# Strassen's seven products for twelve pairs of projected tiles in a one-core hybrid attention and state-space layer

## The chip, the cores and the metric

The kernel runs on one core of one Trainium2 chip. The metric is the device time of one execution in microseconds (us). A core has TensorE (PE, with its weight loads shown apart as PEld), VectorE (DVE), ScalarE (ACT), GpSimd (POOL) and SyncE (SP), whose queue issues nearly all DMAs here. Each engine runs its own instructions in program order and waits on semaphores that the others count up.

## The reference, cut to what matters

```python
u = x * (1.0 + scale[:, None, :]) + shift[:, None, :]
proj = u @ w_in                       # (1024 x 1024) @ (1024 x 5328)
q_lat, kv_lat, z_attn, xbc, dt_raw, z_ssm = split_last(proj, IN_SPLITS)
o_attn = mla_branch(q_lat, kv_lat, ...) * silu(z_attn)
o_ssm = ssd_branch(xbc, dt_raw, z_ssm, ...)   # conv of 4 taps, silu, then 8 chunks of 128 tokens
mixed = concatenate([o_attn, o_ssm]) @ w_out
return layer_norm(DEEPNORM_ALPHA * x + gate * mixed, ln_g, ln_b)
```

All is float32. In `ssd_branch` each chunk of 128 tokens needs exponentials of cumulated decays, products with masks, and the state left by the chunk before it.

## The kernel before, in words

Every float32 product is made as three passes of a split operand: a high part (a copy rounded by ACT) and a low part (raw minus high, by DVE or POOL), high by high, high by low, low by high, summed in PSUM (`three`). The projection has 34 tiles of 128 columns of `w_in`. A tile is turned out for two halves of 512 tokens, each over 8 blocks of the contraction, so it is 2 x 8 x 3 = 48 matmuls of 128x128x512. Tiles 0 to 5 give latents, rope and dt; tiles 6 to 17 are the 12 `xbc` tiles, whose convolution of four taps is made by DVE (`conv`, L1630 to L1673) and whose SiLU is made by ACT; tiles 18 to 33 are 16 gate tiles (z), one for attention and one for the state-space branch per chunk.

The weights of a tile come by SP (`load_tile`, L426) into one of two buffers `wraw`; ACT makes `wh` (`high`, L1178) and POOL makes `wl` (`split_tile`, L661, one 128x1024 subtraction). The z tiles are used as filling work in the eight chunks of the scan: `chunk(c, (2, 6, 4))` on PE (L877) does 2 parts of 8 matmuls, turns the staged chunk (`t_ready`), does 6 parts, the first two y rounds (`y_pair(0)`), 4 parts, the later two y rounds (`y_pair(2)`) and the new states. A y round needs `g_ready`, which ends one of DVE's four rounds.

DVE's program order in a chunk (L1716 to L1752) is: copies of the turned tiles, `xdt`, rounds 0 and 1, the evacuation of y rounds 0 and 1, rounds 2 and 3, `xdte`, evacuations 2 and 3, the state, the copy of the next stage. One round (`ssd_round`, L1686) is: a 128x4 subtraction, a 128x4 copy, four 128x128 instructions that write the exponent's argument (`arg_ready`), the product `cts`, and the product `dec` by `cbs` once ACT has made the exponential (`dec_ready`). ACT's order in a chunk (L1282) is: for rounds 0 and 1 the exponential of the rows (`exp_rows`) and of the decays (`exp_decay`, which waits for `arg_ready`), then two gate halves, the next `wh`, then rounds 2 and 3, two gate halves, the next `wh`. POOL in a chunk: one tile's `wl`, `xd` from the stage and the skip weights once the last chunk's y has been stored (`y_out`), the other tile's `wl`.

After the projection come the eight attention heads and the output projection, which the change leaves in their order.

Of the kernel before, what the change touches and what calls it, by code (L numbers as in the profile page):

```python
# [31 lines left out]
P = 128  # L32
D = 1024
# [34 lines left out]
SERIAL = 26  # L68
SLOT = (0, 1, 2, 3) * 6 + (0, 1, 4, 5, 2, 3, 0, 1)
# [13 lines left out]
def build_layer(nc, x, c, pos, w_ada, b_ada, w_in, qg, w_qb, kvg, w_kvb, conv_w, conv_b, dt_bias,  # L83
# [5 lines left out]
    sco = nc.dram_tensor("attn_scratch", [HEADS, P, S], F32).ap()  # L89

    ctx = ExitStack()
    with ctx:
# [8 lines left out]
        def sem(name):  # L101
# [4 lines left out]
        (ident, ones, mask_qk, mask_ls, colv, modc, gate_b, dsk, dsr, dtb, alg, ccol, rcst, small), end_c = at(base, [  # L106
            ("ident", [P, P], F32), ("ones", [P, P], F32), ("mask_qk", [P, P], F32), ("mask_ls", [P, P], F32),
            ("colv", [P, NVEC], F32), ("modc", [P, 16], F32), ("gate_b", [P, D], F32), ("dsk", [P, NST], F32), ("dsr", [P, SSM_H], F32),
# [4 lines left out]
        limit = nc.sbuf_usable_end  # L113

        (xin,), _ = at(reg_a, [("xin", [P, CHUNKS, D], F32)])
        (cx,), e = at(reg_a, [("cx", [P, 13, S], F32)])
        assert e <= reg_b
# [5 lines left out]
        top = (limit - 3 * S * 4) // 64 * 64  # L123
        (csn, krh, krl), _ = at(top, [("csn", [P, S], F32), ("krh", [P, S], F32R), ("krl", [P, S], F32R)])

        (uh, ul, wraw, wh, wl, ost), b1 = at(reg_b, [
            ("uh", [P, KT, S], F32R), ("ul", [P, KT, S], F32R), ("wraw", [P, 2, KT, P], F32),
            ("wh", [P, 2, KT, P], F32R), ("wl", [P, 2, KT, P], F32R), ("ost", [P, 2, S], F32)])
        (acc, wada, uf, vrow), e = at(b1, [("acc", [P, 2, 3, 2 * P], F32), ("wada", [P, 4, KT, 2 * P], F32),
                                           ("uf", [P, 2, S], F32), ("vrow", [NVEC, P], F32)])  # L130
        assert e <= limit
        (qk, xr, rb), e = at(b1, [("qk", [P, LAT, S], F32), ("xr", [P, 2, S + 4], F32), ("rb", [P, 2, S], F32)])
        assert e <= top

        posi = nc.alloc_sbuf_tensor_at("posi", [P, S], I32, offset=reg_a + 11 * S * 4)
        ropex, ropes, turns, dtv, sqs, dtw = cx[:, 8, :], cx[:, 9, :], xr[:, 0, 0:S], cx[:, 11, :], cx[:, 10, :], rb[:, 1, :]
        (wrx, whx, wlx), e = at(reg_a + 8 * S * 4, [("wrx", [P, KT, P], F32), ("whx", [P, KT, P], F32R), ("wlx", [P, KT, P], F32R)])
        assert e <= reg_a + 11 * S * 4
        (stg, xdt, bdt, cbs, exa, cts, state, xd, cdv, dec, xdte), e = at(b1, [
            ("stg", [P, 13, P], F32), ("xdt", [P, D], F32), ("bdt", [P, B0 + 2 * P], F32),  # L140
            ("cbs", [P, 2 * P], F32), ("exa", [P, 2, HB], F32), ("cts", [P, 2, HB], F32), ("state", [P, D], F32),
            ("xd", [P, NST, P], F32), ("cdv", [P, 3, SSM_H], F32), ("dec", [P, 4, HB], F32), ("xdte", [P, D], F32)])
        assert e - (D + 4 * HB) * 4 >= b1 + (LAT * S + 2 * (S + 4)) * 4
        xdte_at = e - D * 4
        assert e <= top
# [10 lines left out]
        sint = nc.alloc_sbuf_tensor_at("sint", [P, S], F32, offset=top - S * 4)  # L156
        assert e <= top - S * 4 and top - S * 4 >= xdte_at
# [4 lines left out]
        slot_at = [reg_a + q * 2 * (MX + OW) for q in range(3)] + [reg_b, ta_at + 2 * S * 4, top - S * 4]  # L162
# [5 lines left out]
        (res, lgb, lbb, yn, bns, gm), e = at(reg_b + 28 * 1024, [  # L168
            ("res", [P, CHUNKS, D], F32), ("lgb", [P, D], F32), ("lbb", [P, D], F32), ("yn", [P, RT, D], F32),
            ("bns", [P, CHUNKS, 24], F32), ("gm", [P, RT, D], F32)])  # L170
# [51 lines left out]
        colv_mm = sem("colv_mm")  # L222
        colv_ready = sem("colv_ready")
        gate_in = sem("gate_in")
        gate_acc = sem("gate_acc")
        gate_mm = sem("gate_mm")
# [10 lines left out]
        w_split = sem("w_split")  # L237
        proj_ready = sem("proj_ready")
        proj_evac = sem("proj_evac")
        dt_v = sem("dt_v")  # L240
        dt_abs = sem("dt_abs")
        dt_log = sem("dt_log")
# [4 lines left out]
        ss_mm = sem("ss_mm")  # L247
# [10 lines left out]
        acum_out = sem("acum_out")  # L258
# [20 lines left out]
        pos_in = sem("pos_in")  # L279
        pos_read = sem("pos_read")  # L280
        csn_ready = sem("csn_ready")
        csn_arg = sem("csn_arg")
        kr_t = sem("kr_t")
        kr_swapped = sem("kr_swapped")
        kr_sum = sem("kr_sum")
        krh_ready = sem("krh_ready")
        kr_ready = sem("kr_ready")
# [44 lines left out]
        ln_in = sem("ln_in")  # L332
# [44 lines left out]


        @block.sync
        def _(sp):  # L380
            sp.dma_start(ccol[:], c[0].rearrange("(p t) -> p t", t=KT)).then_inc(c_in, 16)

            def small_inputs():
                for dst, src in (
                    (gate_b[:], b_ada[0, 2 * D:3 * D].partition_broadcast(P)),
                    (dsr[:], d_skip[0].partition_broadcast(P)),
                    (rcst[:], const_in),
                    *[(dst[o:o + 16], src[0].rearrange("(h a) -> h a", a=1))
                      for dst, src in ((dtb, dt_bias), (alg, a_log)) for o in range(DT0, P, 16)],
                ):  # L390
                    sp.dma_start(dst, src).then_inc(small_in, 16)
# [4 lines left out]
            def x_columns(k):  # L396
                sp.dma_start(xin[:, :, k * P:(k + 1) * P],
# [20 lines left out]
            small_inputs()  # L418
            sp.dma_start(posi[:], pos[0].partition_broadcast(P)).then_inc(pos_in, 16)
# [5 lines left out]
            def load_tile(p, col, wait):  # L425
                src = w3[:, :, bass.ds(address(col), P)]  # L426
                if wait is not None:
                    sp.wait_ge(w_split, wait)
                sp.dma_start(wraw[:, p], src).then_inc(w_in_sem[p], 16)

            def store_z(tile, p, i):
# [1593 lines left out]
```

## Time and profile before

| | |
|---|---|
| Time, median of 3 runs | 935.5 us (934.63 to 935.82) |
| Span of the profiled execution | 932.6 us, run times lie some 2.9 us above it |
| Granted clock of TensorE, mean | 0.996 of full |
| PE busy | 898.0 us, 96% |
| DVE, ACT, POOL busy | 672.0, 462.3, 216.4 us |
| DMA | 126.27 MB, mean 135 GB/s |

A matmul's row shows its latency, which overlaps the next one's: back to back they start closer together than they last. "Busy" of PE is the time covered by any of them. The releaser named behind an idle time is the last semaphore event by this profile.

### The profile page before, as it was taken

To read this page: it belongs to the slowest core of one execution; us is meant where nothing else is said; L and a number is where in the kernel's file an instruction comes from. 1 tells how busy PE (TensorE), PEld (TensorE's weight loads), DVE (VectorE), ACT (ScalarE), POOL (GpSimd) and SP (SyncE) were. 2 spreads that over 40 slices of the span, in tenths; PEclk is the share of its full clock that TensorE was granted. 3 is DMA by queue.
4 is the path that set the end of the run, shared out by engine and by line. 5 is a ranking of instruction groups with operands and counts; after the bars stand their busy time and mean duration, and the time that the engine had idled before them with its cause. 6 is when DMAs were issued, how large, how long until landed. Compare 5 with 4: busy or idle time off the path is not lost.

```text
span 932.6 us, 13480 instructions
## 1 busy us (share of the span) xinstructions
PE 898.0 (96%) x4737; PEld 747.7 (80%) x4737; DVE 672.0 (72%) x1078; ACT 462.3 (50%) x727; POOL 216.4 (23%) x116
## 2 busy tenths in 40 slices
PE   4999999999999999999989999999999999999995
PEld 3788778788878788877878888888888788888884
DVE  6977489966877677777656766766766758457977
ACT  3654243533544554346457667666675934323421
POOL 1022212322212122121561323413315000002412
PEclk9999999999999999999999999999999999999998
DMA  9973204411234424444660422431422549534611
GB/s 297 320 280 96 63 22 160 112 46 45 66 116 136 140 86 134 135 135 127 178 215 15 147 64 88 147 105 44 146 104 90 181 154 407 194 135 152 204 51 79
DMA packets 110044, 126.27 MB, mean 135 GB/s; under 512 B 10646, under 2 KB 84599, under 8 KB 110007
## 3 DMA queue, kind: packets, MB, share of 16 engines
q1 hardware_dynamic: 109600, 124.95, 41.5%
q10 hardware_dynamic: 406, 0.84, 0.3%
q8 instruction: 22, 0.36, 0.2%
q14 instruction: 16, 0.12, 0.0%
HBM read 93.98 MB, written 27.85 MB: 131 GB/s over the span
## 4 chain that ended last, share of the span: by engine, by line
PE 71%; issue 12%; DVE 6%; SPq 5%; ACT 3%; POOL 1%; DMA 1%; DVEq 0%; ACTq 0%; POOLq 0%
PE bank L856 17%; PE bank L755 13%; PE bank L757 12%; PE bank L756 12%; PE bank L994 3%; SPq L404 2%; PE bank L979 2%; PE bank L873 2%; PE bank L983 2%; PE bank L982 2%; PE bank L980 2%; PE bank L981 2%; POOL wl L664 1%; PE bank L910 1%; PE bank L875 1%
## 5 line engine op out<-in xcount | busy, mean ns | idle before, releaser
L664 POOL TENSOR_TENSOR wl<-wraw,wh 128x1024 fp32r<-128x1024 f32 x31 | 78.1, 2520 | 199.0 <-ACT wh L1182 199.0
L755 PE MATMUL bank<-uh,wh 128*128 128x512 f32 x272 | 107.9, 397 | 2.8 <-DVE ul L1534 2.2
L756 PE MATMUL bank<-ul,wh 128*128 128x512 f32 x272 | 106.1, 390 | 0.0
L757 PE MATMUL bank<-uh,wl 128*128 128x512 f32 x272 | 106.0, 390 | 0.0
L856 PE MATMUL bank<-uh,wh 128*128 128x512 f32 x256 | 102.7, 401 | 0.0
L856 PE MATMUL bank<-ul,wh 128*128 128x512 f32 x256 | 101.2, 395 | 0.0
L755 PE MATMUL bank<-owh,mxh 128*128 128x512 f32 x256 | 100.1, 391 | 0.0
L856 PE MATMUL bank<-uh,wl 128*128 128x512 f32 x256 | 99.9, 390 | 0.0
L757 PE MATMUL bank<-owh,mxl 128*128 128x512 f32 x256 | 99.7, 390 | 0.0
L756 PE MATMUL bank<-owl,mxh 128*128 128x512 f32 x256 | 99.7, 389 | 0.0
L1280 ACT ACTIVATE dec<-dec 128x512 f32<-128x512 f32 x32 | 20.3, 633 | 113.1 <-DVE dec L1695 113.1
L1365 ACT ACTIVATE prob<-bank,small 128x1024 f32<-128x1024 f32 (+3 forms) x64 | 47.5, 743 | 34.2 <-DVE small L1798 34.0
L1840 DVE TENSOR_TENSOR owl<-owr,owh 128x1024 fp32r<-128x1024 f32 x32 | 41.0, 1280 | 32.6 <-ACT owh L1408 32.6
L755 PEld LDWEIGHTS bank<-uh,wh 128*128 128x128 f32 x272 | 51.3, 189 | 15.0 <-DVE ul L1534 3.1
L1811 DVE TENSOR_TENSOR ptl<-bank,pth 128x512 fp32r<-128x512 f32 (+1 forms) x96 | 50.2, 551 | 16.2 <-ACT pth L1384 15.8
L757 PEld LDWEIGHTS bank<-uh,wl 128*128 128x128 f32 x272 | 51.2, 188 | 10.7
L756 PEld LDWEIGHTS bank<-ul,wh 128*128 128x128 f32 x272 | 51.2, 188 | 10.7 <-issue 0.5
L1408 ACT ACTIVATE owh<-owr 128x1024 fp32r<-128x1024 f32 x32 | 33.8, 1057 | 50.9 <-PE bank L757 34.8
L856 PEld LDWEIGHTS bank<-ul,wh 128*128 128x128 f32 x256 | 48.1, 188 | 12.5 <-issue 3.0
L856 PEld LDWEIGHTS bank<-uh,wh 128*128 128x128 f32 x256 | 48.1, 188 | 11.5 <-issue 1.7
L755 PEld LDWEIGHTS bank<-owh,mxh 128*128 128x128 f32 x256 | 48.1, 188 | 10.3 <-DVE mxl L1842 0.3
L757 PEld LDWEIGHTS bank<-owh,mxl 128*128 128x128 f32 x256 | 48.0, 188 | 10.1
(231 smaller groups left out, 2207.7 us busy)
## 6 DMA issues: line engine op xcount, KB each, us to landing
wraw<-in_w_in SPq DMA_DIRECT2D x33, 512.0 KB, 3.7
owr<-in_w_out SPq DMA_DIRECT2D x32, 512.0 KB, 4.6
wada<-in_w_ada SPq DMA_DIRECT2D x16, 512.0 KB, 6.0
dec<-acum_scratch SPq DMA_DIRECT2D x32, 256.0 KB, 3.8
proj_scratch<-ost SPq DMA_DIRECT2D x16, 512.0 KB, 4.7
xin<-in_x SPq DMA_DIRECT2D x8, 512.0 KB, 6.0
cx<-in_w_ada SPq DMA_DIRECT2D x1, 4096.0 KB, 16.7
ssm_scratch<-xd SPq DMA_DIRECT2D x8, 512.0 KB, 5.4
```

The lines of the kernel that those rows point to most:

```text
L404: sp.dma_start(wada[:, k % 4, :, part * P:(part + 1) * P], ada[:, :, part, k, :]).then_inc(ada_in[k % 4], 16)
L664: pool.tensor_tensor(wl[:, p], wraw[:, p], wh[:, p].bitcast(F32), ALU.subtract).then_inc(w_split, 1)
L755: pe.matmul(dst, ah, bh, start=start, stop=False)
L756: pe.matmul(dst, ah, bl, start=False, stop=False)
L757: return pe.matmul(dst, al, bh, start=False, stop=stop)
L856: mm = pe.matmul(bk(2 * p + n), a[:, p, k, :], b[:, k, n * HB:(n + 1) * HB], start=(k == 0 and q == 0), stop=(k == KT - 1 and q == 2))
L994: mm = pe.transpose(bk(4 + n % 2)[:, (t - t0) * P:(t - t0 + 1) * P], prob[:, i % 2, t * P:(t + 1) * P], ident[:])
L1280: act.activation(dec[:, r, :], dec[:, r, :], ACT.Exp).then_inc(dec_ready, 1)
L1365: act.activation(prob[:, i % 2, 0:n], score_view(i), ACT.Exp, bias=small[:, 8 + i % 2:9 + i % 2], accum_out=small[:, 12 + i % 2:13 + i % 2 ...
L1408: act.activation(owh[at][:], owr[q][:], ACT.Copy).then_inc(e_hi, 1)
L1811: dve.tensor_tensor(ptl[:, t0:t0 + w, q], bk(4 + n % 2)[:, 0:w * P].rearrange("p (t q) -> p t q", q=P), pth[:, t0:t0 + w, q].bitcast(F32), ...
L1840: dve.tensor_tensor(owl[at][:], owr[q][:], owh[at][:].bitcast(F32), ALU.subtract).then_inc(e_split, 1)
```

## The change

Products are made after Strassen's scheme for 12 pairs of tiles: the last 8 `xbc` tiles as 4 pairs (q = 0 to 3), and the z tiles of a chunk as one pair (q = 4 to 11). Tiles 0 to 9 stay as they were. A pair is a 2x2 block product: two halves of the contraction and the two tiles on the weight side; two halves of the contraction and the two halves of the tokens on the other. It has 7 products of 4 blocks x 3 passes = 12 matmuls each, 84 in all, where two tiles had 96. The differences of u are made once, by DVE, and split by ACT and POOL (`split_difference`, four of 128x2048). For each pair POOL makes four sums of weights and seven low parts, all 128x512, and ACT seven high parts.

Products 0, 2, 4 and 6 (counted from 0) add up in one PSUM bank, which ACT copies out between them; 3 and 5 do so in another; DVE adds products 1, 4 and 5 from PSUM to what ACT has copied. So PE waits, between products of a pair, for ACT's copies and DVE's additions:

```diff
+            def product(i, q, odd):
+                pe.wait_ge(pair_split, 7 * q + i + 1)
...
+                elif i == 2:
+                    pe.wait_ge(prod_copied, 4 * q + 1)
...
+                elif i == 4:
+                    pe.wait_ge(prod_copied, 4 * q + 2)
+                elif i == 5:
+                    pe.wait_ge(prod_copied, 4 * q + 3)
+                elif isinstance(q, int) and q < PAIRS_XBC:
+                    pe.wait_ge(prod_added, 3 * q + 2)
+                else:
+                    pe.wait_ge(prod_added, 3 * q + 1)
```

Here `prod_copied` 4q + 2 is the copy of product 2, and `prod_added` 3q + 1 in a z pair is the addition of product 4. PE's chunk becomes:

```diff
+                product(0, q, odd)
...
+                turn_stage(c)
+                if not first:
+                    product(1, q, odd)
+                product(2, q, odd)
+                product(3, q, odd)
+                product(4, q, odd)
...
+                y_pair(0, c)
+                product(5, q, odd)
+                product(6, q, odd)
+                y_pair(2, c)
+                if more:
+                    new_states(c)
```

ACT's chunk (in chunk 0 the copy of product 0 and the first high part stand ahead of the row exponentials):

```diff
+                exp_rows(0, c)
+                exp_rows(1, c)
+                if not first:
+                    act.wait_ge(z_out[0], 16 * c)
+                    copy_product(0, q, odd, ost[:, 0, halves[0]])
+                if more and not first:
+                    high_product(0, q + 1)
+                exp_decay(0, c)
+                exp_rows(2, c)
+                exp_rows(3, c)
+                exp_decay(1, c)
+                if more:
+                    high_product(1, q + 1)
...
+                copy_product(2, q, odd, ost[:, 0, halves[1]])
...
+                copy_product(3, q, odd, ost[:, 1, halves[1]])
+                if more:
+                    high_product(2, q + 1)
+                    high_product(3, q + 1)
+                exp_decay(2, c)
...
+                exp_decay(3, c)
```

It goes on with the small exponential, high parts 4 and 5, two gate SiLUs once all three additions are done, the SiLU of product 6 and high part 6. In the last chunk latents stand in place of high part 1. DVE's chunk:

```diff
+                ssd_round(0, c)
+                ssd_round(1, c)
...
+                ssd_round(2, c)
                 y_out_round(0, c)
                 y_out_round(1, c)
-                ssd_round(2, c)
                 ssd_round(3, c)
+                add_product(4, q, odd, ost[:, 1, halves[1]])
```

then `xdte`, the additions of products 1 and 5, evacuations 2 and 3 and the state. `cts` is written in place of the row exponentials, which have four buffers. POOL, for each pair, with `skip_rows` (the old `xd`) behind it in every chunk:

```diff
+                pool.tensor_tensor(s1, a21, a22, ALU.add).then_inc(pair_sum, 1)
+                pool.wait_ge(pair_sum, 4 * q + 1)
+                pool.tensor_tensor(s2, s1, a11, ALU.subtract).then_inc(pair_sum, 1)
+                split_product(0, q, a11)
+                pool.tensor_tensor(a11, a11, a21, ALU.subtract).then_inc(pair_sum, 1)
+                split_product(1, q, a12)
+                pool.wait_ge(pair_sum, 4 * q + 2)
+                pool.tensor_tensor(a12, a12, s2, ALU.subtract).then_inc(pair_sum, 1)
+                split_product(2, q, s2)
+                split_product(3, q, s1)
```

and low parts 4, 5 and 6. A low part waits for its high part. SP loads both tiles of pair q + 1 once low parts 5 and 6 of pair q are made.

Around this, memory is laid out anew. The convolved tiles go to memory outside the chip (`scx`) and each chunk's stage is loaded from there by SP, in place of DVE's copy; the rope tables, the split rope keys and the gate go there and back as well. Convolution uses four buffers. The last two `xbc` tiles end so on DVE, and the first z pair's weights follow on SP:

```diff
+                if q == PAIRS_XBC - 1:
+                    dve.wait_ge(prod_copied, 4 * q + 4)
+                    conv(j + 1, 0, P)
+                    conv(j, HB, S)
...
+                    dve.tensor_copy(stg[:, LAST_Y, :], conv_out(LAST_Y)[:, 0:P]).then_inc(stage_ready, 1)
+                    conv(j + 1, P, S)
...
+            store_conv(LAST_X)
+            store_conv(LAST_Y)
             with sp.Fori(0, CHUNKS - 1) as i:
...
+                load_pair(i + PAIRS_XBC + 1)
```

In pair q = 0 DVE makes five latent norms between the additions of products 1 and 4. At the end of the last chunk the latents are loaded and split once products 1 to 4 have freed the memory in which u stood.

## Rows read from the trace of the kernel before

**Rows 1.** The page's first part: span; busy time, share and instructions of each engine.
```profile
span 932.6 us, 13480 instructions
PE 898.0 (96%) x4737; PEld 747.7 (80%) x4737; DVE 672.0 (72%) x1078; ACT 462.3 (50%) x727; POOL 216.4 (23%) x116
```

**Rows 2.** Stretches of convolution and of chunks: length, busy time by engine, clock, DMA.
```profile
123.00:238.00 115.00, 114.42 (x502) 93.17 (x501) 93.33 (x59) 46.97 (x54) 27.88 (x11) 1.00 0.27 79
238.00:471.00 233.00, 231.39 (x1415) 186.48 (x1414) 167.82 (x352) 117.08 (x157) 60.27 (x28) 1.00 0.43 128
```

**Rows 3.** Timeline of PE in one chunk: start, duration, engine, line, operation, tiles.
```profile
354.85 1.04 PE L893 MATMUL bank<-ident,stg 128*128 128x128 f32 x8
...
356.42 0.48 PE L856 MATMUL bank<-ul,wh 128*128 128x512 f32 x1
...
367.18 0.39 PE L856 MATMUL bank<-uh,wh 128*128 128x512 f32 x1
...
369.40 0.50 PE L856 MATMUL bank<-ul,wh 128*128 128x512 f32 x1
```

**Rows 4.** Timeline of DVE in the same chunk and at the next one's start.
```profile
356.70 0.49 DVE L1718 COPY bdt<-bank 128x320 f32<-128x320 f32 x1 [2.24 <-PE bank L897]
...
358.63 1.79 DVE L1689 TENSOR_TENSOR cdv<-dec,bdt 128x4 f32<-128x4 f32 x1
...
360.46 1.14 DVE L1695 SCALAR_TENSOR_TENSOR dec<-dec,bdt,mask_ls 128x128 f32<-128x128 f32 x4
...
363.10 1.14 DVE L1695 SCALAR_TENSOR_TENSOR dec<-dec,bdt,mask_ls 128x128 f32<-128x128 f32 x4
...
386.12 0.49 DVE L1718 COPY bdt<-bank 128x320 f32<-128x320 f32 x1 [2.24 <-PE bank L897]
```

**Rows 5.** Timeline of POOL in the same chunk.
```profile
356.16 1.90 POOL L686 TENSOR_TENSOR xd<-stg,dsk 128x1024 f32<-128x1024 f32 x1 [14.84 <-DMA ssm_scratch<-xd]
358.01 2.39 POOL L664 TENSOR_TENSOR wl<-wraw,wh 128x1024 fp32r<-128x1024 f32 x1
```

**Rows 6.** Timeline of all engines in the last chunk, third round.
```profile
462.54 3.28 DVE L1695 SCALAR_TENSOR_TENSOR dec<-dec,bdt,mask_ls 128x128 f32<-128x128 f32 x4
...
463.25 2.42 POOL L699 TENSOR_TENSOR qll<-wraw,qlh 128x1024 fp32r<-128x1024 f32 x1 [3.50 <-ACT qlh L1329]
```

**Rows 7.** Timeline of all engines in the output projection.
```profile
854.58 1.54 DVE L1840 TENSOR_TENSOR owl<-owr,owh 128x1024 fp32r<-128x1024 f32 x1 [2.26 <-ACT owh L1408]
855.12 2.15 POOL L720 TENSOR_TENSOR yn<-yn,lbb 128x512 f32<-128x512 f32 x1
856.05 1.77 DVE L1842 TENSOR_TENSOR mxl<-mxr,mxh 128x512 fp32r<-128x512 f32 x1
```

**Rows 8.** POOL by line and shape: count, busy us, mean ns, idle before.
```profile
L693 POOL TENSOR_TENSOR hwl<-hwr,hwh 128x512 fp32r<-128x512 f32 x4 | 5.2, 1288 | 11.8 <-ACT hwh L1324 11.8
```

**Rows 9.** Timeline of ACT in the same chunk as rows 3.
```profile
364.28 0.63 ACT L1280 ACTIVATE dec<-dec 128x512 f32<-128x512 f32 x1 [1.49 <-DVE dec L1695]
364.93 1.28 ACT L1272 ACT_TABLE_LOAD   x1
366.22 1.09 ACT L1272 ACTIVATE ost<-bank 128x512 f32<-128x512 f32 x2
```

**Rows 10.** The page's DMA issues: transfer, queue, count, KB each, us to landing.
```profile
wraw<-in_w_in SPq DMA_DIRECT2D x33, 512.0 KB, 3.7
...
ssm_scratch<-xd SPq DMA_DIRECT2D x8, 512.0 KB, 5.4
```

**Rows 11.** Timeline of DVE in the convolution's opening.
```profile
129.90 2.61 DVE L1636 SCALAR_TENSOR_TENSOR cx<-xr,colv,cx 128x1024 f32<-128x1024 f32 x2
...
136.09 13.14 DVE L1645 RECIPROCAL rb<-rb 128x1024 f32<-128x1024 f32 x2 [2.26 <-ACT rb L1235]
149.27 6.44 DVE L1648 SCALAR_TENSOR_TENSOR qk<-qk,colv,rb 128x1024 f32<-128x1024 f32 x5
```

**Rows 12.** A stretch behind PE's last matmul, columns as in rows 2.
```profile
924.00:928.00 4.00, 0.00 (x0) 0.00 (x0) 3.86 (x7) 0.29 (x1) 0.32 (x1) 0.61 0.32 131
```

More of the change, by code:

```diff
@@ new lines, in _ @@
+            load_pair(0)
+            store_conv(0)
+            store_conv(1)
+            load_pair(1)
+            for i, t in enumerate((2, 3, 4, 0, 1)):
+                sp.wait_ge(lat_ready, i + 1)
+                sp.dma_start(scr[t], qk[:, t, :]).then_inc(y_out, 16)
+            store_conv(2)
+            store_conv(3)
+            for q in range(2, PAIRS_XBC + 1):
+                load_pair(q)
+                for j in range(2):
+                    store_conv(2 * q + j)
+            sp.wait_ge(decay_out, 96)
@@ L861, in y_pair @@
+            for q in range(PAIRS_XBC):
+                for i in range(7):
+                    product(i, q, q % 2 == 1)
             def y_pair(r0, c):
@@ L874, in y_pair, with turn_stage @@
                         for q in range(2):
-                            mm = pe.matmul(d[q], state[:, own[q]], cts[:, r % 2, of[q]], start=False, stop=True)
+                            mm = pe.matmul(d[q], state[:, own[q]], decays(r)[:, of[q]], start=False, stop=True)
                     mm.then_inc(y_ready, 1)
-            def chunk(c, fills):
-                parts = iter([(p, n, part) for p in range(2) for n in range(2) for part in range(3)])
-                assert sum(fills) == 12
-                def fill(count):
-                    for _ in range(count):
-                        p, n, part = next(parts)
-                        proj_part(p, n, part, 2 * c + 18 + p)
-                fill(fills[0])
-                pe.wait_ge(stage_ready, c + 1)
-                if not isinstance(c, int) or c > 0:
+            def turn_stage(c):
+                pe.wait_ge(stg_in, 16 * c + 32)
+                if isinstance(c, int) and c == 0:
+                    pe.wait_ge(stage_ready, 1)
+                else:
                     pe.wait_ge(state_new, c + 1)
@@ new lines, in copy_product, with conv_silu @@
+            def copy_product(i, q, odd, dst):
+                act.wait_ge(prod_ready, 7 * q + i + 1)
+                act.activation(dst, {0: bk(3) if odd else bk(0), 2: bk(3) if odd else bk(0), 3: bk(2),
+                                     6: bk(3) if odd else bk(0)}[i], ACT.Copy).then_inc(prod_copied, 1)
+            def conv_silu(j):
+                act.wait_ge(conv_done, j + 1)
+                act.activation(conv_out(j), conv_out(j), ACT.Silu).then_inc(silu_done, 1)
+            halves = [slice(n * HB, (n + 1) * HB) for n in range(NHALF)]
@@ L1259, in _ @@
[L1259 to L1272 removed]
+            high_difference(2)
@@ L1280, in exp_decay, with z_gates @@
                 act.activation(dec[:, r, :], dec[:, r, :], ACT.Exp).then_inc(dec_ready, 1)
-            def chunk(c, more):
-                exp_rows(0, c)
+            def z_gates(q, c, odd, n):
+                if n == 0:
+                    act.wait_ge(prod_added, 3 * q + 3)
+                    act.activation(ost[:, 0, :], ost[:, 0, :], ACT.Silu).then_inc(z_done, 1)
+                    act.activation(ost[:, 1, halves[1]], ost[:, 1, halves[1]], ACT.Silu)
+                else:
+                    act.wait_ge(prod_ready, 7 * q + 7)
+                    act.activation(ost[:, 1, halves[0]], bk(3) if odd else bk(0), ACT.Silu).then_inc(prod_copied, 1)
@@ L1297, in chunk @@
[L1297 to L1302 removed]
+                if more:
+                    high_product(1, q + 1)
+                else:
+                    act.wait_ge(prod_ready, 7 * PAIRS - 5)
+                    latent_high(0)
+                    latent_high(1)
+                copy_product(2, q, odd, ost[:, 0, halves[1]])
```

978 lines of the change are left out of this document (594 added, 384 removed).

## The prediction

> **What bounds the kernel now.** I read the first part of the page, then the busy times by stretch, then the timelines of one chunk. PE is busy 898.0 of 932.6 us [rows 1], and in the stretches that the change touches 114.42 of 115 and 231.39 of 233 us [rows 2]. No other engine comes near. So matmuls taken out are worth their whole pitch, as long as nothing that now hides behind them comes due. That second half of the sentence decides this case: the reader should look in the timelines for how much DVE, ACT and POOL have in hand behind each product, and what they do to each other.
>
> **What is removed.** 48 matmuls run from 356.42 to 367.18 us [rows 3]: 10.76 / 47 = 0.229 us each (the 0.39 of a row is latency). Twelve pairs lose 12 matmuls each: 144 x 0.229 = 33.0 us, 2.75 us a pair. With all else hidden the time would be 935.5 - 33 = 902.5 us. A product is 12 x 0.229 = 2.75 us. A chunk lasts 386.12 - 356.70 = 29.4 us now [rows 4] and its work on PE will be 26.7.
>
> **What is added.** POOL: 11 instructions of 128x512 for a pair in place of two of 128x1024. The nearest row gives 1.29 us for a subtraction of that shape [rows 8], so 14.2 us a pair, and in a chunk 1.90 more for the skip rows [rows 5]: 16.1, against some 6.7 now. ACT: the high parts cost the same columns, plus three copies and SiLUs of what was evacuated anyway; it has room. DVE: three additions of 512 from PSUM, less the copy of the stage. By share all this fits under 26.7 us. By lock it does not:
>
> *POOL and DVE exclude each other.* The 128x4 subtraction on DVE at 358.63 lasts 1.79 us, to 360.42, just as POOL's instruction ends at 360.40 [rows 4, 5]; a 128x128 one needs 1.14 / 4 = 0.29, so 1.6 or so of it is waiting. Four 128x128 instructions of one round last 1.14 us alone [rows 4] and 3.28 with a POOL instruction of 2.42 that got in between the third and the fourth [rows 6]. And they take turns: DVE's at 854.58 waits for POOL's first, POOL's of 855.12 waits for DVE and lasts 2.15 instead of 1.29, DVE's next one waits for that, 1.77 us [rows 7]. DVE's evacuation from PSUM runs beside POOL unhindered. So where POOL has a row of instructions ready, each short DVE instruction with both inputs in SBUF waits for one of them, about 1.2 us. DVE's four rounds take 4 x 2.64 = 10.6 us of such work (360.46 to 363.10 is one round [rows 4]); with POOL's 16.1 that is 26.7, the whole chunk.
>
> The Trainium skill (SBUF — State Buffer, "Who interferes with whom") has this as an exclusive lock between GpSimd and DVE instructions with two SBUF inputs, held for the whole instruction; it says that whoever issues first has it, and nothing of turns. Taken as a lock that costs only where instructions happen to meet, it would make this kernel rival B below; with the turns of rows 7 it makes the forecast.
>
> **A middle chunk, step by step**, from the end of the turned stage, T.
> PE has products 1 to 3 until T + 8.2; then product 4 waits for ACT's copy of product 2. In ACT's order that stands behind `exp_decay(1)`, which waits for the arguments of DVE's round 1, and behind high part 1. From DVE's first copy to the end of those arguments is 364.24 - 356.70 = 7.5 us today, the wait of 1.6 for POOL included [rows 4, 5]; that block stays, since POOL still waits for y's store, 5.4 us [rows 10], and so starts when the stage is turned. Exponential 0.63, high part and copy 0.55 each [rows 9]: copy 2 ends at T + 9.3, 1.1 us late. That much is sure. Now the turns: the next pair's weights have landed by then (3.7 us [rows 10] after low parts made at the end of the last chunk), so POOL goes from the skip rows straight into four instructions (two sums, low part 0, a difference) until it lacks high part 1. All four fall into rounds 0 and 1: 4 x 1.2 = 4.8 us. I take both ends' upper one here, since nothing else is left for POOL to do: stall 5.9 us.
> Product 6 waits for the addition of product 4, which now stands behind rounds 2 and 3 and the evacuation of y rounds 0 and 1. Without POOL: round 1 done T + 8.9, round 2 T + 11.6, first y rounds (1.99 us [rows 3]) end T + 14.1, evacuated 14.9, round 3 17.5, addition 18.2; PE is done with product 5 at 16.8: 1.4 us late. With four more turns (low part 1, a difference, low parts 2 and 3) it is 3.7; a part of them falls into DVE's wait for y, so I take 3.0.
> A middle chunk: 26.7 + 5.9 + 3.0 = 35.6 us, 6.2 more than now; six of them: +37.
>
> **Chunk 0.** Once pair 3's last product is done, DVE still has about one and a half convolutions in pieces (1.3 us for each of three steps of 1024 columns [rows 11], a whole one some 4.7), stage copies between: estimate 9.6 us, and SiLU 1. Only then SP may store that tile and fetch the next weights, 0.4 + 3.7 [rows 10]; ACT waits for these at high part 0, which stands ahead of the row exponentials. High part, table load 1.28, exponential [rows 9], two rounds' arguments 3.9, then exponential, high part, copy: 23.7 us. PE has four products and the turning, 12.6. Stall 11.1, plus turns 4.8, plus 3.0 at product 6, less 2.75: +16.2.
> **Chunk 7.** No next pair, but two latents of 1.1 us each (twice 0.55) ahead of copy 2: stall 2.5 + 2.0 - 2.75 = +1.8.
> **The way out.** Latents and their weights are split while PE runs products 5 and 6 only; the tables come from outside the chip. 0 to 8, I take 3.
>
> **The convolution's pairs.** Four save 11.0 us. In pair 0, product 6 needs DVE's addition of product 4, behind convolution 2, a reciprocal (6.6), convolution 3 and five norms, 6.4 [rows 11]: 23.8 us plus 3.5 until ACT gets to tile 8, against 27.5 that PE has (tile 9 and six products). It just fits; but eleven of DVE's instructions there can each lose a turn to POOL, which splits u's differences and two pairs in that time: 0 to 13.2, I take 10. Later pairs have slack of several us. Sum: -1.
>
> **Sum.** -1 + 16.2 + 37.2 + 1.8 + 3 = +57 us. Span 932.6 + 57.2 = 989.8; with the 2.9 by which the run lies above the profiled span, 992.7. The input stage and the attention keep their order: at nothing, covered by PE's unbroken work; In front of tile 6 DVE has the four differences of u (2.6 us each, estimate from the 1.3 for 1024 columns [rows 11]), ten steps of the rope tables (some 11), eight gate terms (10.4) and some 7 of dt and rope: 39 us, against tiles 2 to 5 on PE, 4 x 11.0 = 44. I take it as hidden; with POOL's turns it could cost some 5.
>
> **Rivals.**
> A, the forecast: turns at the lock on the way to copy 2. 993 us, chance 0.55.
> B, on the other side: POOL's instructions meet DVE's only by chance, so only the late copy and addition remain. Middle chunks 26.7 + 1.1 + 1.4 = 29.2 (-0.2 x 6), chunk 0 +9.8, chunk 7 +1.1, convolution -11, way out 0: -1.3 in all, 934 us. For it: DVE idles in places into which POOL may fall. Against it: rows 7. It decides from less than one lost turn a chunk on. Chance 0.18, in which faster and slower are about even.
> C, also on the other side: copies and additions come in time, the saving stays whole: 903 us. It would need ACT to reach copy 2 some 1.1 us before DVE's rounds let it. 0.15.
> D: the stalls of A let TensorE's clock fall. Behind the last matmul, at 922.7, the granted clock of 924 to 928 us averages 0.61 [rows 12], so it went to its lower level, 1.2 GHz, after some 2 us of rest. A product at that level costs 2.75 us more; in each of eight chunks, 22: 1015 us. 0.12.
>
> **Numbers.** 993 us. The range leaves out C and the far ends of B and D: 920 to 1025. A difference of 0.2% is about what a measurement of this kernel can tell. Faster by more: C and half of B, 0.23; within it 0.05; slower 0.72.
>
> **What would show it.** PE's longest waits: product 4 for ACT's copy, some 6 us each in chunks 1 to 6; then product 6 for DVE's addition, about 3. DVE's 128x128 and 128x4 instructions with means far above 0.3 us, POOL's 128x512 above 1.29. Chunks 35 to 36 us apart. Product 6 of the first pair late by some 10. In chunk 0 ACT waits for a weight load. Wrong would be: chunks of 29 us with those means undisturbed (B); no wait on `prod_copied` at all (C); a clock under 1 in the chunks (D); or a hole before tile 6 or the attention, which I have at next to nothing.

## The result: slower by 7.6%, and the profile after

| | before | after |
|---|---|---|
| Time, median | 935.7 us (934.63 to 935.82) | 1006.1 us (1004.05 to 1009.89) |
| Ratio, 95% interval | | 1.0759 (1.0734 to 1.0784) |
| Span of the profiled execution | 932.6 us | 1002.2 us |
| Mean granted clock | 0.996 | 0.963 |

After, first part of the page and its clock by slices (to be held against [rows 1]):

```profile
span 1002.2 us, 13509 instructions
PE 899.3 (90%) x4593; PEld 737.1 (74%) x4593; DVE 763.5 (76%) x1117; ACT 473.7 (47%) x785; POOL 386.2 (39%) x228
PEclk9999997899788999999998999999999999999998
```

144 matmuls fewer, and PE is busy as long as before: what it does runs slower in the middle. After, by stretch (length, busy time and count of PE, PEld, DVE, ACT, POOL, granted clock, DMA share, GB/s); against [rows 2]:

```profile
51.00:123.00 72.00, 71.91 (x309) 57.75 (x308) 65.29 (x50) 30.33 (x36) 29.47 (x11) 1.00 0.53 169
123.00:263.50 140.50, 116.97 (x475) 93.49 (x474) 115.83 (x79) 51.97 (x76) 106.17 (x59) 0.92 0.37 108
263.50:302.40 38.90, 27.95 (x156) 21.36 (x156) 26.98 (x48) 17.29 (x27) 15.83 (x11) 0.81 0.38 115
337.20:371.30 34.10, 28.91 (x169) 22.39 (x168) 28.38 (x47) 14.77 (x24) 18.20 (x12) 0.95 0.45 134
```

A chunk begins where DVE copies the turned tiles. By these marks the 69.6 us divide so:

| stretch | before | after | more | predicted |
|---|---|---|---|---|
| start to chunk 0 | 240.98 | 263.56 | +22.6 | -1 |
| chunk 0 | 27.5 | 38.8 | +11.4 | +16.2 |
| chunks 1 to 6 | 6 x 29.42 | 6 x 34.2 | +28.8 | +37 |
| from chunk 7 on | 487.6 | 494.6 | +6.9 | +4.8 |

(Chunk 0's mark stands behind 24 matmuls of its pair after and 16 of its tiles before, so some 1.8 us of the first line belong to the second.) Up to 123 us nothing is lost, as forecast: PE is busy 71.91 of 72.

PE's longest waits behind the input stage; the first two are those that the prediction named (engine, line, what for; us in all, times, longest):

```profile
PE bank L932 <- ACT ost L1435: 35.3, 8, 10.0
PE bank L932 <- DVE ost L1973: 11.3, 8, 3.6
PE bank L932 <- ACT xrb L1435: 9.6, 3, 5.9
PE bank L1091 <- DMA stg<-conv_scratch: 6.2, 1, 6.2
```

L1435 is ACT's copy of a product, L1973 DVE's addition. In a middle chunk product 4 waits 4.2 us for the first, product 6 waits 1.0 for the second. But a list of waits says who was waited for, not what it would bring to shorten one. That is in the chain of waits, followed back from the end. After, one chunk of it (start, us, what; some pieces, all under 1.3 us, are left out):

```profile
339.79 1.15 DVE dec L2031 x4
340.96 0.64 ACT dec L1545
342.24 1.26 DVE cdv L2025
343.60 4.20 DVE dec L2031 x4
347.82 0.64 ACT dec L1545
349.10 1.26 DVE cdv L2025
350.46 4.12 DVE dec L2031 x4
354.60 0.64 ACT dec L1545
356.79 1.15 DVE dec L2031 x4
357.97 0.64 ACT dec L1545
359.24 0.69 DVE ost L1973
359.98 0.50 PE bank L932
```

No product is in it before product 6, at 359.98: from the turned stage (337.17) on, the chain is DVE's four rounds, then the addition of product 4: 22.8 us. L2031 are the four 128x128 instructions of a round (the rounds are counted from 0): 1.15 us undisturbed, 4.2 in rounds 1 and 2, and the 128x4 copy ahead of them (L2025) 1.26 instead of 0.16. POOL in the same stretch:

```profile
341.72 1.75 POOL L821 TENSOR_TENSOR wxy<-wraw 128x512 f32<-128x512 f32 x1 [2.05 <-DMA wraw<-in_w_in]
343.55 1.29 POOL L823 TENSOR_TENSOR wxy<-wxy,wraw 128x512 f32<-128x512 f32 x1
344.80 1.32 POOL L814 TENSOR_TENSOR wl<-wraw,wh 128x512 fp32r<-128x512 f32 x1
346.08 1.31 POOL L825 TENSOR_TENSOR wraw<-wraw 128x512 f32<-128x512 f32 x1
349.05 1.28 POOL L814 TENSOR_TENSOR wl<-wraw,wh 128x512 fp32r<-128x512 f32 x1 [1.67 <-ACT wh L1430]
350.29 1.28 POOL L828 TENSOR_TENSOR wraw<-wraw,wxy 128x512 f32<-128x512 f32 x1
```

Eight instructions of POOL, in two rows of four (the last two, to 354.1, are not shown), beside two of DVE's rounds: two copies and two times four arguments lose 1.1 + 1.1 + 3.05 + 2.97 = 8.2 us, and 8.6 with the 0.4 that the skip rows cost the first copy. In each row one instruction of POOL holds up the copy and the next three hold up three of the four arguments. That is a turn of about 1.0 us for each instruction of POOL.

### The profile page after: what moved, and what is told of

Read it like the earlier page. It is cut to its first block, busy times and chain, and to the rows that moved or that the text cites. A ratio compares the mean times of both kernels' runs of the same rounds, so it can differ in the third digit from the quotient of the medians.

```text
span 1002.2 us, 13509 instructions
## 1 busy us (share of the span) xinstructions
PE 899.3 (90%) x4593; PEld 737.1 (74%) x4593; DVE 763.5 (76%) x1117; ACT 473.7 (47%) x785; POOL 386.2 (39%) x228
## 4 chain that ended last, share of the span: by engine, by line
PE 56%; DVE 23%; issue 6%; ACT 6%; SPq 4%; DMA 3%; POOL 2%; DVEq 0%; ACTq 0%; POOLq 0%
PE bank L932 14%; PE bank L934 14%; PE bank L933 14%; DVE dec L2031 8%; PE bank L1209 3%; DVE cvb L1954 2%; ACT dec L1545 2%; SPq L470 2%; DVE cdv L2025 2%; PE bank L1194 2%; PE bank L1198 1%; PE bank L1197 1%; PE bank L1195 1%; POOL diff_lo L804 1%; PE bank L1196 1%
## 5 line engine op out<-in xcount | busy, mean ns | idle before, releaser
L932 PE MATMUL bank<-uspan,wh 128*128 128x512 f32 x352 | 147.0, 418 | 18.2 <-DVE ost L1973 11.3
L934 PE MATMUL bank<-uspan,wl 128*128 128x512 f32 x352 | 139.6, 397 | 0.0
L814 POOL TENSOR_TENSOR wl<-wraw,wh 128x512 fp32r<-128x512 f32 x60 | 102.6, 1721 | 74.1 <-ACT wh L1430 74.1
L933 PE MATMUL bank<-uspan,wh 128*128 128x512 f32 x304 | 119.1, 392 | 0.0
L932 PE MATMUL bank<-diff_hi,wh 128*128 128x512 f32 x144 | 65.0, 451 | 46.6 <-ACT ost L1435 35.3
L932 PEld LDWEIGHTS bank<-uspan,wh 128*128 128x128 f32 x352 | 67.5, 192 | 40.6 <-issue 15.6
L2031 DVE SCALAR_TENSOR_TENSOR dec<-dec,bdt,mask_ls 128x128 f32<-128x128 f32 x128 | 83.9, 715 | 1.1
L933 PE MATMUL bank<-diff_lo,wh 128*128 128x512 f32 x192 | 84.4, 439 | 0.0
L934 PEld LDWEIGHTS bank<-uspan,wl 128*128 128x128 f32 x352 | 67.5, 192 | 15.0
L933 PEld LDWEIGHTS bank<-uspan,wh 128*128 128x128 f32 x304 | 57.6, 189 | 13.1 <-issue 2.2
L934 PE MATMUL bank<-diff_hi,wl 128*128 128x512 f32 x144 | 63.1, 438 | 0.0
L1430 ACT ACTIVATE wh<-wraw 128x512 fp32r<-128x512 f32 x60 | 36.3, 623 | 56.6 <-DMA wraw<-in_w_in 45.9
L1653 ACT ACTIVATE prob<-bank,small 128x1024 f32<-128x1024 f32 (+3 forms) x64 | 47.6, 744 | 32.4 <-DVE small L2145 32.1
```

The source lines that it names most:

```text
L814: pool.tensor_tensor(wl[:, at], part, wh[:, at].bitcast(F32), ALU.subtract).then_inc(pair_split, 1)
L932: pe.matmul(dst, ah, bh, start=start, stop=False, skip_group_check=running)
L933: pe.matmul(dst, ah, bl, start=False, stop=False, skip_group_check=running)
L934: return pe.matmul(dst, al, bh, start=False, stop=stop, skip_group_check=running)
L1430: act.activation(wh[:, PRODUCT_SLOT[i]], part, ACT.Copy).then_inc(pair_high, 1)
L1653: act.activation(prob[:, i % 2, 0:n], score_view(i), ACT.Exp, bias=small[:, 8 + i % 2:9 + i % 2], accum_out=small[:, 12 + i % 2:13 + i % 2 ...
```

## Experiments

The question after this reading was what bounds a chunk: the waits that one sees on PE (my sum), or the chain on DVE. Each kernel below was timed beside the kernel before on the same chip (medians of that 934.4 to 936.3); ratios are to it.

### Does the place of ACT's copy matter?

```diff
                 exp_rows(3, c)
+                copy_product(2, q, odd, ost[:, 0, halves[1]])
                 exp_decay(1, c)
...
-                copy_product(2, q, odd, ost[:, 0, halves[1]])
```

> ACT's copy of product 2 stands ahead of exp_decay(1) and of the next high part. Program-order theory (product 4 is late because of where its copy stands, as the sum of the prediction has it): the 4.2 us in front of product 4 go, in chunks 1 to 6 and in part in 0 and 7; with the slow clock behind it (about 1.7 us) that is some 5 to 6 us a chunk, 1006 becomes about 965. Chain theory (product 6 waits for DVE's addition of product 4, which ends 22.8 us after the turned stage whatever PE does, since DVE's rounds with POOL's turns fill that time): the idle time moves to the first y rounds and to product 6, chunks stay 34.1 us apart, 1003 to 1006.

1020.6 us, ratio 1.0906 (1.0882 to 1.0929): slower than after by 14 us, where both theories had it at 1006 or faster. PE in a chunk, and two windows (the chunk, and behind product 6's wait):

```profile
389.19 0.44 PE L1078 MATMUL bank<-dec,xdt 128*64 128x128 f32 x4 [0.63 <-DVE dec L2039]
399.93 0.79 PE L932 MATMUL bank<-uspan,wh 128*128 128x512 f32 x1 [6.71 <-DVE ost L1973]
376.65:414.00 37.35, 30.01 (x168) 23.27 (x167) 28.82 (x46) 14.87 (x24) 17.38 (x12) 0.86 0.39 122
402.00:406.00 4.00, 4.00 (x15) 2.77 (x15) 0.80 (x2) 2.12 (x4) 0.75 (x1) 0.50 0.26 105
```

The wait of 4.2 us is gone, and product 6 starts 23.3 us after the turned stage (22.8 in after): the program-order theory falls, the chain stands. What the chain theory didn't have is the loss. One rest of 6.7 us now stands in front of work that is on the chain, and that work, product 6 and the later y rounds, runs at a granted clock of 0.50, the level of 1.2 GHz: from product 6 to the next turned stage it takes 14.1 us here and 11.3 in after. In after, the rest that let the clock fall stood in front of product 4, which had time.

### Are the turns bound to the rounds, or to chance?

```diff
+                if not (isinstance(q, int) and q <= PAIRS_XBC):
+                    pool.wait_ge(arg_ready, 4 * (q - PAIRS_XBC) - 2)
                 pool.wait_ge(w_in_sem[0], 16 * q + 80)
```

> POOL starts on the next pair's weights only when DVE has written the exponents' arguments of round 1. Turns theory: the four arguments of round 1 take 1.14 us again in place of 4.2, product 4 waits about 1.1 us in place of 4.2; but the same instructions of POOL now meet rounds 2 and 3, whose arguments take about 4.1 us each, and the addition of product 4 ends as late as before: product 6 waits some 4 us, chunks about 34 us apart, 1000 to 1010. Chance theory (a meeting costs only where two instructions happen to overlap): half the stretched instructions go and don't come back, chunks 30 to 31, about 985.

1019.1 us, 1.0887 (1.0867 to 1.0907). DVE's arguments of rounds 1 and 2, and product 6 of that chunk:

```profile
383.55 1.14 DVE L2033 SCALAR_TENSOR_TENSOR dec<-dec,bdt,mask_ls 128x128 f32<-128x128 f32 x4
388.27 5.14 DVE L2033 SCALAR_TENSOR_TENSOR dec<-dec,bdt,mask_ls 128x128 f32<-128x128 f32 x4
400.80 0.80 PE L934 MATMUL bank<-uspan,wh 128*128 128x512 f32 x1 [6.54 <-DVE ost L1975]
```

Round 1 is free (1.14), round 2 pays for both: its four arguments take 5.14 us, its products 1.77 and 1.75 instead of 0.69. Turns theory held in kind: nothing was given back. The size was missed (1000 to 1010 expected): all the waiting now gathers in one rest of 6.5 us, as in copy2_early.

### Is the low clock a cost of its own?

```diff
-                for k in range(4):
+                for k in [k for n in range(times) for k in range(4)]:
...
-                product(3, q, odd)
+                product(3, q, odd, 2)
```

> Product 3 is made twice in every chunk (its second pass starts the bank anew), so PE rests 1.4 instead of 4.2 us in front of product 4, with 12 more matmuls a chunk. If the lower TensorE clock is a term of the loss by itself (product 4 takes 4.5 us at a granted clock of 0.60 instead of 2.75): 1.7 us a chunk come back, 1006 becomes about 993. Chain theory: product 4 is back at 2.75 us, but product 6 still starts when DVE's addition is done, so its wait grows from 1.0 to about 2.7 us and chunks stay at 34.1: 1004 to 1006.

1008.1 us, 1.0771 (1.0753 to 1.0789), after plus 2 us: no gain. In the middle chunk:

```profile
339.00:373.20 34.20, 29.94 (x180) 23.47 (x179) 28.54 (x46) 14.77 (x24) 18.32 (x12) 1.00 0.42 133
361.99 0.50 PE L932 MATMUL bank<-uspan,wh 128*128 128x512 f32 x1 [2.63 <-DVE ost L1973]
```

The clock is back at 1.00, PE does 12 matmuls more, and the chunk lasts 34.2 us as before; product 6 waits 2.6 instead of 1.0. In after's chunks the slow clock costs nothing.

### What is POOL's work worth?

```diff
-                pool.tensor_tensor(wl[:, at], part, wh[:, at].bitcast(F32), ALU.subtract).then_inc(pair_split, 1)
+                f = cut(q)
+                pool.tensor_tensor(f(wl[:, at]), f(part), f(wh[:, at].bitcast(F32)), ALU.subtract).then_inc(pair_split, 1)
```

`cut` takes 8 of every 128 columns, in the four sums too; pair 0 stays whole. The kernel leaves out the other columns of sums and low parts.

> POOL's sums and low parts of pairs 1 to 11 are made for 8 of every 128 columns only; their number, order and semaphores stay. The rest of the weights' low parts is left out, so this isn't the reference's output. Turns theory: DVE's stretched instructions (8.6 us in a middle chunk beyond their time alone) go; the chain to the addition of product 4 is then 14.2 us and PE decides: 26.7 us plus about 1.1 in front of product 4 = 27.8, six times 6.3 less, with what chunks 0, 1 and 7 and the convolution's pairs give another 10 to 20: 945 to 960. If another wait bounds the chunk (the weight loads, ACT's order), chunks stay above 32 us and the time above 985.

951.9 us, 1.0160 (1.0138 to 1.0181): 54 us less than after. Arguments take 1.14 us again, and a middle chunk is:

```profile
343.14:371.55 28.41, 27.30 (x168) 21.27 (x167) 19.98 (x46) 14.68 (x24) 6.68 (x12) 1.00 0.53 157
```

28.4 us, and the stage of chunk 0 is turned 11.5 us earlier (248.5 against 260.0): POOL's columns cost 5.7 us in a chunk and 11.5 in the convolution. Three of POOL's instructions, of 0.25 to 0.30 us now, run beside DVE's four arguments of round 1, and these take 1.14 us all the same.

The other side of it is the old kernel with that load, 6 and 5 instructions of 128x512 for a chunk's two tiles, and nothing else of the change:

```diff
-                split_tile(0, 2 * i + 18)
+                split_pieces(0, 2 * i + 18, 9 * (i - 1), 6)
...
-                split_tile(1, 2 * i + 19)
+                split_pieces(1, 2 * i + 19, 9 * (i - 1) + 5, 5)
```

> The kernel before, with POOL making each later z tile's low part in pieces of 128x512, some of them again with the same result: 11 instructions of 128x512 for a chunk in place of two of 128x1024, the load on POOL of the change without its products, copies and additions. Turns theory: DVE's rounds 2 and 3 end 23.6 us after the turned stage (19.5 and 4.1 us of turns) where PE is ready for the later y rounds at 20.1: about 3.5 us a chunk, seven chunks, 936 becomes about 960. Chance theory: less than 1 us a chunk, 936 to 942.

982.4 us, 1.0498 (1.0481 to 1.0516): +47 us with not one product changed, where the turns theory expected 24 and chance at most 6. POOL's row, DVE's arguments of rounds 0 and 1 beside and behind it, PE in front of the later y rounds, and the chunk:

```profile
310.25 6.38 POOL L669 TENSOR_TENSOR wl<-wraw,wh 128x512 fp32r<-128x512 f32 x5
312.84 4.20 DVE L1708 SCALAR_TENSOR_TENSOR dec<-dec,bdt,mask_ls 128x128 f32<-128x128 f32 x4
318.54 1.14 DVE L1708 SCALAR_TENSOR_TENSOR dec<-dec,bdt,mask_ls 128x128 f32<-128x128 f32 x4
333.02 0.44 PE L886 MATMUL bank<-dec,xdt 128*64 128x128 f32 x4 [2.22 <-DVE dec L1719]
335.66 0.45 PE L886 MATMUL bank<-dec,xdt 128*64 128x128 f32 x4 [1.54 <-DVE dec L1719]
310.55:345.68 35.13, 31.37 (x180) 24.59 (x179) 26.98 (x45) 14.12 (x19) 15.80 (x13) 0.95 0.33 104
```

4.20 against 1.14 within two rounds of one chunk is the turn as plain as it gets. PE waits 2.2 + 1.5 = 3.8 us, as expected (3.5); on top the clock falls in front of the new states and the next tiles, which are on the chain: PE is busy 31.4 us in this chunk, and 32.1 on average of chunks 1 to 6 (which lie 35.8 apart), with what took 29.4 at full clock. That part the expectation lacked.

### Can the order be mended?

add4_early takes both waits out of the products' way, with copies 2 and 3 and the addition of product 4 made earlier:

```diff
+                add_product(4, q, odd, ost[:, 1, halves[1]])
                 ssd_round(2, c)
                 y_out_round(0, c)
                 y_out_round(1, c)
                 ssd_round(3, c)
-                add_product(4, q, odd, ost[:, 1, halves[1]])
...
+                copy_product(2, q, odd, ost[:, 0, halves[1]])
+                if not first:
+                    act.wait_ge(z_out[1], 16 * c)
                 exp_decay(1, c)
+                copy_product(3, q, odd, ost[:, 1, halves[1]])
```

> In every chunk copies 2 and 3 stand ahead of the next high parts (copy 2 ahead of exp_decay(1)) and DVE adds product 4 between rounds 1 and 2 instead of behind round 3. This takes product 6 off the chain through rounds 2 and 3. Chain theory: the addition ends about 13 us after the turned stage instead of 22.8, product 6 waits for nothing; what is late next is round 3 for the later y rounds, some 23.3 us after the turned stage against 19.4 of PE: a rest of about 4 us there, chunks 31.7 us apart (up to 33 if the lower clock falls on the work behind it), six times 1 to 2.4 less than 34.1: 990 to 1000. If the addition was not what bound the chunk, no change: 1004 to 1008; if the longer single rest costs clock as in copy2_early, above 1010.

989.5 us, 1.0581 (1.0563 to 1.0599), just under the 990 to 1000 that were expected: 16.7 us less than after. Chunks are 32.2 us apart on average (from 297.41 to 490.70, six); there the products wait no more, the y rounds do, for DVE's rounds. Two of its chunks:

```profile
362.39:397.18 34.79, 30.26 (x168) 23.07 (x167) 29.20 (x47) 15.25 (x25) 18.30 (x13) 0.90 0.49 162
397.18:427.05 29.87, 27.24 (x168) 21.36 (x167) 27.35 (x47) 14.38 (x24) 16.99 (x12) 1.00 0.36 119
```

The same code: 3.0 of the 4.9 us between them are PE's work at the lower clock.

chunk0_order, in chunk 0 alone:

```diff
                 if first:
                     copy_product(0, q, odd, ost[:, 0, halves[0]])
-                    high_product(0, q + 1)
...
                 exp_decay(1, c)
+                if first:
+                    copy_product(2, q, odd, ost[:, 0, halves[1]])
+                    high_product(0, q + 1)
```

> In chunk 0 alone ACT makes high part 0 of the next pair behind the exponentials of round 1 and behind copy 2, so the load of that pair's weights doesn't hold up the rows' exponentials. In after these stood behind a wait of 5.8 us, and product 4 waited 10.0. By the prediction's step for chunk 0: the wait goes to 2 to 4 us, chunk 0 lasts some 6 to 8 us less, 998 to 1000. Rival (DVE's rounds meet POOL's turns later and the addition of product 4 sets chunk 0's end too): 1 to 3 us kept, 1003 to 1005.

1005.5 us, 1.0750 (1.0722 to 1.0779), no difference that the time shows. In chunk 0 product 4's wait falls from 9.98 to 1.2 us, product 6's grows from 0.97 to 7.0: the rival, again a wait that moves to DVE's addition. From chunk 0 to chunk 7 it is 241.1 against 244.1 us.

Two orders for the convolution, which the prediction had at next to nothing. conv_order:

```diff
                 copy_product(0, q, odd, one[:, halves[0]])
+                copy_product(2, q, odd, one[:, halves[1]])
+                act.wait_ge(conv_done, LATE if q == 0 else j - 2)
+                copy_product(3, q, odd, two[:, halves[1]])
                 high_product(0, q + 1)
                 high_product(1, q + 1)
...
                 add_product(4, q, odd, two[:, halves[1]])
+                if q == 0:
+                    for t in (2, 3, 4, 0, 1):
+                        latent_norm(t)
```

> In the convolution's pairs ACT makes copies 2 and 3 ahead of the next pair's high parts 0 to 2, and DVE adds product 4 of pair 0 ahead of the five norms of the latents instead of behind them. Chain theory: product 6 of pair 0 started at 179.3 us because the norms (10.2 us with POOL's turns) stood ahead of that addition; it starts 8 us earlier now, the waits of 5.9 and 2.0 us go, but DVE's work up to the last convolution is the same and it has only some 15 us of holes in that stretch, so 4 to 8 us are kept: 998 to 1002. Rival (DVE and POOL are the bound of the whole stretch, not single waits): nothing is kept, 1005 to 1007, and the first stage is turned at 260 us as before. Rival 2 (the high parts were late already): the next pairs' low parts come late and it is slower than 1007.

1012.5 us, 1.0832 (1.0810 to 1.0855): 6 us more. What was saved in pair 0 came back in pair 1:

```profile
193.90 0.77 PE L932 MATMUL bank<-diff_hi,wh 128*128 128x512 f32 x1 [10.28 <-ACT xra L1435]
```

ACT's copy there waits for a buffer that DVE clears only once the latents are stored, and these came later.

opening, in the first pair:

```diff
-            for i in range(3):
+            for i in range(2):
                 high_product(i, 0)
             act.wait_ge(conv_done, 1)
             evac(8, conv_in(2)[:, 3:3 + S])
+            high_product(2, 0)
...
                 copy_product(0, q, odd, one[:, halves[0]])
+                if q == 0:
+                    copy_product(2, q, odd, one[:, halves[1]])
                 high_product(0, q + 1)
...
-                if isinstance(q, int) and q == 0:
-                    split_difference(3)
                 pool.wait_ge(pair_sum, 4 * q + 4)
                 split_product(5, q, a12)
                 split_product(6, q, a22)
+                if isinstance(q, int) and q == 0:
+                    split_difference(3)
```

> Three moves in the first pair of the convolution alone: ACT evacuates tile 8 ahead of high part 2 (which waited 6.3 us for POOL's second sum while DVE waited 4.2 us for that tile), POOL makes low parts 5 and 6 ahead of u's fourth difference (4.6 us, so the next pair's weights are fetched that much earlier), and ACT makes copy 2 ahead of the next pair's high parts, which waited 11.6 us for those weights. Chain theory: the waits of 3.0 and 5.9 us in front of products 2 and 4 of pair 0 fall to 0 and about 2, part of the lower clock behind them goes too, and 5 to 9 us are kept: 997 to 1001. Rival (DVE's norms in front of the addition of product 4, and the one set of weight buffers that each pair must free before the next can be fetched, keep the pace): product 6 of pair 0 and all later pairs stand where they stood, 1004 to 1007.

1008.9 us (1001.54 to 1010.45), 1.0758 (1.0714 to 1.0802): nothing. Product 6 of pair 0 starts at 181.8 (179.3 in after) and now waits 4.8 us for the addition behind the norms. Then the edits together: add4_early and chunk0_order, in all_orders with conv_order, in best_orders with opening in its place:

> The three edits of conv_order, chunk0_order and add4_early together. If each removes another stretch's chain they add up: 1006 less about 6, 7 and 12 = 981. With none of POOL's work taken away it stays well above the kernel before; if the gains overlap, 985 to 995.

> The edits of opening, chunk0_order and add4_early together. add4_early took 16.8 us off the eight chunks, chunk0_order 3.0; with 5 to 9 from the opening: 1006 less 25 to 29 = 977 to 981. If the opening gives nothing, 984 to 987.

995.3 us, 1.0654 (1.0637 to 1.0672), and 986.1 us, 1.0535 (1.0517 to 1.0553). conv_order costs in company too, 9 us against opening. best_orders, where opening gives nothing as before, is the fastest whole version, 20 us under after and 51 over before. Last, whether any such order could have won: best_orders, with POOL's columns left out as in pool_small.

> best_orders with POOL's sums and low parts of pairs 1 to 11 made for 8 of every 128 columns, as in pool_small: the rest of the low parts is left out, so this isn't the reference's output. It asks what the scheme could give if POOL's work cost DVE nothing. pool_small took 951.9 us; opening and orders take 5 to 9 us from its first pair and up to 1 us from each chunk of 28.4: 935 to 945, so no gain worth the name over the kernel before. If the three convolution pairs behind the first then run at PE's pace as well, 925 to 935.

937.4 us, 1.0020 (1.0005 to 1.0034). Two chunks of it:

```profile
304.79:331.49 26.70, 26.70 (x168) 21.43 (x167) 20.44 (x47) 14.75 (x24) 5.91 (x12) 1.00 0.48 161
331.49:358.19 26.70, 26.70 (x168) 21.42 (x167) 20.85 (x47) 14.93 (x25) 5.91 (x12) 1.00 0.58 177
```

26.70 against 29.42 us: here the saving stands whole, 2.72 us a pair. And still it is no gain: chunk 0 begins at 253.1 instead of 241.0, and behind the mark of chunk 7 it takes 498.0 us instead of 487.6.

## Where the prediction was right and where wrong

**Sign and main cause: right. Size: right with luck.** 993 was forecast, 1006 measured, inside the range. But chunks 0 to 6 had 53 us in the sum and measure 42, while the convolution had -1 and measures 21 or more; two errors in opposite directions make the total look better than its terms. The turns at the lock are shown from both sides: without most of POOL's columns 54 us go, and POOL's load alone, in the old kernel, brings 47 (the whole change brings 70, its saving of 33 taken off).

**The price of removed matmuls: right.** 2.75 us a pair forecast, 2.72 in best_small. Rival C needed nothing else to come due. best_small takes away most of POOL's work, and even so the rest of the change eats the gain.

**The middle chunk: right engine, wrong sum.** I forecast 35.6 us and it is 34.2. Product 4 waits 4.2 instead of 5.9: the four turns before it cost 4.1 us and not 4.8, and the skip rows hold up DVE for 0.4 and not 1.6, so that the copy would not be late without turns. Product 6 waits 1.0 instead of 3.0. The step that failed is the addition itself: 26.7 + 5.9 + 3.0 adds PE's waits as if each could be had back. Nor do the waits as measured give the chunk: 26.7 + 4.2 + 1.0 = 31.9, and the other 2.2 us are PE at its lower clock, busy 28.9 us with work of 26.7. The true account is one chain: 22.8 us from the turned stage to DVE's addition of product 4, then product 6, y rounds, new states, product 0 and the turning, 11.3. "That much is sure", of the copy 1.1 us late, was wrong: in pool_small, without turns, product 4 waits 0.2 to 0.3 us. Its opposite number, the addition of product 4 behind round 3, 1.4 by my steps, is 0.9 there. Rival B's chunk of 29.2 is 28.4.

**Rival D: the clock.** It did fall, to 0.60 in the stretch of product 4, which takes 4.5 instead of 2.75 us, behind a rest of 4.2; the "some 2 us of rest" that I read from rows 12 are not enough in a chunk, where a rest of 2.6 in warm leaves the clock at 1.00. Of its price, 22 us added to the forecast, warm leaves nothing in the chunks: the slow product sits beside the chain. The step that failed is again that it was added. Where a rest stands on the chain the price is real, as copy2_early (14 us) and before_pool (2 to 3 a chunk) show, and in the convolution after, below.

**Chunk 0: 13 with the share of the mark, for 16.2.** The wait in front of product 4 is 10.0 and ACT waits 5.8 us for weights, as described (the pieces that I listed for ACT's path add up to 22.8 us, not to the 23.7 that I used). Not in my steps: PE waits 6.2 us in front of the turning, ahead of chunk 0's mark and so in the first line of the table, since the stage now comes back from memory outside the chip, through the queue and two transfers. I had let DVE's copy of the stage go as a gain and priced its stand-in at nothing.

**The convolution: the term that was mis-sized, -1 forecast, +21 to +23 measured.** PE's account of 123 to 263.5 us: what it had to do, 117.4 less 11.0 plus 1.8 = 108.2; idle 23.5; the rest, 8.8, is PE at a clock of 0.92. Idle in pair 0:

```profile
155.46 0.50 PE L932 MATMUL bank<-diff_hi,wh 128*128 128x512 f32 x1 [2.98 <-ACT xrb L1435]
166.93 0.63 ACT L1430 ACTIVATE wh<-wraw 128x512 fp32r<-128x512 f32 x1 [11.61 <-DMA wraw<-in_w_in]
168.71 0.77 PE L932 MATMUL bank<-diff_hi,wh 128*128 128x512 f32 x1 [5.94 <-ACT xrb L1435]
168.41 10.18 DVE L1965 SCALAR_TENSOR_TENSOR qk<-qk,colv,rb 128x1024 f32<-128x1024 f32 x5
179.33 0.48 PE L932 MATMUL bank<-uspan,wh 128*128 128x512 f32 x1 [2.00 <-DVE xrb L1973]
```

I counted product 6 alone, at 10 us, and these rows are 10.9. So that term was right in size by luck, with the place wrong: over half of it, 5.9 us, is ACT's copy 2 behind a high part that waits for weights. What was missing is all else: "later pairs have slack of several us", which the lock ate (a convolution step of DVE's takes 2.17 us instead of 1.28 where POOL has work, the norms 10.18 instead of 6.44 [rows 11], and POOL's 128x512 beside the norms take 2.15 to 2.27 instead of 1.29, so here both sides pay; DVE is busy 115.8 of 140.5 us); the stage's 6.2; the clock. pool_small gives 11.8 us back of this stretch. That leaves some 11 for orders, transfers and clock, and neither of my two orders got any of it. Which wait holds it is open; both moved a wait to DVE's side, so I take DVE's whole row of work there as the likeliest bound, which was not shown.

**From chunk 7 on: +6.9 for 4.8.** Products 4 and 6 wait 1.4 and 3.6 us in chunk 7, and PE 0.9 and 1.1 later, at a latent's low part and at the attention's start; pool_small, which leaves the latents' split whole, takes as long here as after; the weights' lock beside the latents was not taken apart.

## What to carry to other kernels

Before adding up waits of the bounding engine, follow the chain of waits through one period and ask of every wait what would come next if it were gone: three of these experiments (copy2_early, pool_late, chunk0_order) removed a wait of 4 to 9 us and got nothing, or less. Taking work off a full engine is worth it only if what it costs the helpers is off their chain too; here 2.7 us of PE a pair were bought with 8 us of DVE. In such a kernel look for stretches in which POOL's long instructions don't meet DVE's short chained ones (none that was free showed here: pool_late only moved the meeting), and try the helper's new load alone in the old kernel first: that one run (before_pool, +47 us against 33 to be saved) would have decided this case. Giving the sums and low parts to DVE itself was not tried; at the 0.68 us of its 128x512 rows, eleven would take 7.5 us a pair (an estimate), about what the turns cost it.

## What the runs showed of the hardware that I had not expected

- A turn costs a DVE instruction with one input too: the 128x4 copy takes 1.26 us instead of 0.16 behind POOL, as dear as a 128x128 one. The Trainium skill (SBUF — State Buffer, "Who interferes with whom") says that a copy can enter a mode that takes the shared ports; the trace agrees. DVE's addition with one input in PSUM keeps its 0.68 us in all 24 cases of z pairs.
- With a row of instructions ready on both sides the two engines alternate one by one: four of DVE's, 0.29 us each, take 4.2 us with three of POOL's 1.3 between them and 5.14 with four (pool_late). What DVE loses goes with POOL's length: against instructions of 0.25 to 0.30 us (pool_small) the same four take 1.14. Whether the same columns in smaller pieces would cost DVE less was not tried.
- Two rests of 1.6 and 2.6 us in a chunk leave the clock at 1.00 (warm), one of 6.7 us puts it at the level of 1.2 GHz for more than 4 us of work (copy2_early). Where a rest falls changes a chunk by some 3 us for that alone.
